# The last expert tile taken into the loop, its rows spread by 0/1 matrices on four row groups

## The reference, cut to what matters

```python
# hier_moe: top-1 of 4 expert groups, then top-2 of its 4 experts: two experts of 16 for every token
for g in range(N_EXPERT_GROUPS):
    a = jnp.einsum('btd,edf->btef', h, w1[g])            # 1024 -> 512
    b = jnp.einsum('btd,edf->btef', h, w3[g])
    hid = jax.nn.silu(a) * b * comb[:, :, g, :, None]    # comb: the weight of the token for the expert
    out = out + jnp.einsum('btef,efd->btd', hid, w2[g])  # 512 -> 1024
x = x + gt2 * out                                        # gate gt2, per channel
y = rmsnorm(x, normf_g)
```

## Time and profile before

| what | value |
| --- | --- |
| median of 3 runs | 1212.12 us |
| the profiled execution, its own time | 1218.64 us |
| its span in the trace | 1216.8 us |
| expert stage, from the first L1238 to the end of the span | 893.4 to 1216.8 us |
| loads of weights at full rate | about 912 to 1162 us |
| PE busy over the whole span | 95% |
| DVE busy over the whole span | 44% |

### The profile page before, as it was taken

How to read it: one execution, slowest core, us unless ns; L and a number is a source line. 1 busy time by engine, 2 the same in 40 slices (tenths; PEclk the granted TensorE clock), 3 DMA queues, 4 the chain that set the end, 5 groups by cost and what they waited for, 6 DMA issues and landing times.

```text
span 1216.8 us, 28304 instructions
## 1 busy us (share of the span) xinstructions
PE 1156.2 (95%) x11779; PEld 935.9 (77%) x11779; DVE 540.7 (44%) x1249; ACT 378.7 (31%) x680; POOL 176.9 (15%) x277
## 2 busy tenths in 40 slices
PE   3898999999999999999989999999989999999986
PEld 2687889888899898988759999999755655555542
DVE  1743555565655654553254434357741221111117
ACT  5422333232333332332044444432411222222113
POOL 0343344344444000000000000000030000000030
PEclk9999999999999999999979999999979999999998
DMA  9999878768846589666887888386559999999974
GB/s 310 360 337 369 313 264 317 269 229 278 300 168 224 185 330 333 208 218 237 323 319 279 287 299 291 90 241 255 210 208 397 410 398 394 390 397 382 392 202 116
DMA packets 169763, 350.63 MB, mean 288 GB/s; under 512 B 12179, under 2 KB 116779, under 8 KB 159398
## 3 DMA queue, kind: packets, MB, share of 16 engines
q1 hardware_dynamic: 156230, 326.84, 74.1%
q0 software_dynamic: 6304, 14.57, 4.1%
q10 hardware_dynamic: 7152, 8.13, 2.5%
HBM read 320.08 MB, written 117.50 MB: 360 GB/s over the span
## 4 chain that ended last, share of the span: by engine, by line
PE 75%; DMA 15%; DVE 5%; ACT 2%; issue 2%; ACTq 0%; SPq 0%; DVEq 0%
PE psum L886 44%; DMA xg<-x_rows 11%; PE psum L1238 7%; PE psum L1253 4%; PE psum L962 3%; PE psum L948 2%; PE psum L937 2%; PE psum L928 2%; PE psum L827 2%; PE psum L984 1%; DMA kvr<-in_cache_v_dram 1%; DMA wraw<-in_w_in_dram 1%; PE psum L1011 1%; PE psum L1230 1%; DMA adar<-in_w_ada_dram 1%
## 5 line engine op out<-in xcount | busy, mean ns | idle before, releaser
L886 PE MATMUL psum<-hHi,whi 128*128 128x272 f32 x1216 | 359.0, 295 | 2.1 <-DVE hLo L1639 2.0
L886 PE MATMUL psum<-hLo,whi 128*128 128x272 f32 x1216 | 351.5, 289 | 0.0
L886 PE MATMUL psum<-hHi,wlo 128*128 128x272 f32 x1216 | 349.7, 288 | 0.0
L886 PEld LDWEIGHTS psum<-hHi,whi 128*128 128x128 f32 x1216 | 229.1, 188 | 21.2 <-issue 16.4
L886 PEld LDWEIGHTS psum<-hHi,wlo 128*128 128x128 f32 x1216 | 229.4, 189 | 0.0
L886 PEld LDWEIGHTS psum<-hLo,whi 128*128 128x128 f32 x1216 | 228.7, 188 | 0.0
L1238 PE MATMUL psum<-e,xs 128*32 128x256 f32 x3072 | 179.4, 385 | 4.0 <-issue 2.6
L1591 DVE TENSOR_TENSOR wlo<-wraw,whi 128x1024 fp32r<-128x1024 f32 x100 | 131.9, 1323 | 73.7 <-ACT whi L1354 73.4
L1238 PEld LDWEIGHTS psum<-e,xs 128*32 128x32 f32 x3072 | 101.0, 111 | 73.6 <-issue 11.4
L1354 ACT ACTIVATE whi<-wraw 128x1024 fp32r<-128x1024 f32 x100 | 104.7, 1051 | 34.1 <-PE psum L886 21.5
L1253 PE MATMUL psum<-e,hT 128*32 128x256 f32 x1440 | 83.9, 381 | 0.0
(11 more groups left out here) (365 smaller groups left out, 1726.0 us busy)
## 6 DMA issues: line engine op xcount, KB each, us to landing
e<-in_w_dram SPq DMA_DIRECT2D x48, 2048.0 KB, 15.1
wraw<-in_w_in_dram SPq DMA_DIRECT2D x76, 512.0 KB, 5.4
out_dram<-in_cache_k_dram SPq DMA_DIRECT2D x32, 1022.0 KB, 9.4
out_dram<-in_cache_v_dram SPq DMA_DIRECT2D x32, 1022.0 KB, 7.8
adar<-in_w_ada_dram SPq DMA_DIRECT2D x36, 512.0 KB, 6.9
kvr<-in_cache_k_dram SPq DMA_DIRECT2D x8, 2048.0 KB, 9.2
kvr<-in_cache_v_dram SPq DMA_DIRECT2D x8, 2048.0 KB, 7.7
x_rows<-zrow SPq DMA_DIRECT2D x7, 1170.0 KB, 12.3
```

Of the source, the lines that this page charges most:

```text
L886: mm = pe.matmul(psum[:, t, 0:HALF], w[:, slot, k, :], x[:, k, cols], start=(k == 0 and n == 0), stop=(k == k_n - 1 and n == 2))
```

## The change

Every tile runs in the loop (`Fori(0, pairs)`), the last one too. The store of `yq` moves from the end of a tile to the start of the next one, one slot further on in `y_rows`; so tile 0 stores zeros, and the last tile's result is never stored. The 0/1 matrix is now `placeq`, made in every tile, for the three row groups of the tile and on all 128 partitions, whose four quarters hold the same rows. At the end each sum is made of 12 matmuls of 32 rows and 256 columns, one for each row group and column quarter; quarter c lies in partitions 32c to 32c+31 and goes to a PSUM bank of its own. A sum takes four half-used banks, so two fit at once.

```diff
 SP, before the loop
-            sp.dma_start(place[:, :], k_small[0:TS, 96 + TS:96 + TS + NT]).then_inc(late_in, 16)
+            sp.dma_start(tokens[:, :], k_small[:, 96 + TS:96 + TS + NT]).then_inc(late_in, 16)
 SP, behind the loop
+            sp.wait_ge(spread_pe, 2 * pairs)
+            sp.sem_inc(xg_in[0], 16)
 PE
-            def tile(jp, q, last=False):
+            def tile(jp, q):
-                pe.wait_ge(weigh_done, 10 * jp + (5 * q + 1))
+                pe.wait_ge(weigh_done, 18 * jp + (9 * q + 1))
...
-                if last:
-                    hidden_T(jp, q, 2)
-                    pe.wait_ge(e2_in[q], 16 * jp + 16)
-                    pe.wait_ge(hT_done, 6 * jp + (3 * q + 3))
-                    for n in range(2):
-                        for fc in range(FC):
-                            mm = pe.matmul(psum[0:TS, 6 + n, :], hT[:, fc, :],
-                                           e2[q][:, fc, 512 * n:512 * n + 512], start=(fc == 0), stop=(fc == FC - 1))
-                        mm.then_inc(ye_pe, 1)
-                    return
...
-            with pe.Fori(0, before_last) as jp:
+            with pe.Fori(0, pairs) as jp:
                 for q in range(2):
                     tile(jp, q)
-            tile(before_last, 0)
-            tile(before_last, 1, last=True)
+            pe.wait_ge(weigh_done, 18 * pairs + 1)
+            pe.wait_ge(xs_done, 2 * pairs + 1)
+            pe.wait_ge(ye_ev, 6 * pairs + 3)
+            pe.sem_inc(y_pe, 1)
             for i, tt in enumerate(LAST_ORDER):
                 n = P if tt < TILES else NS
-                if i == 4:
-                    pe.wait_ge(f_gate, 1)
-                if i >= 3:
+                if i >= 2:
+                    pe.wait_ge(f_mix, i - 1)
+                more = () if i < 2 else (ya[:, 1, 0], ya[:, 1, 1]) if i == 2 else (x2[:, tt, :],)
+                for g in range(TG):
+                    for c in range(4):
+                        part = slice(32 * c, 32 * c + 32)
+                        mm = pe.matmul(summed(i)[0:n, c, :], placeq[part, g, P * tt:P * tt + n], yq[part, g, :], start=(g == 0),
+                                       stop=(g == TG - 1 and not more))
+                if more:
                     pe.wait_ge(yg_in[tt], 32)
-                for c in range(2):
-                    cols = slice(512 * c, 512 * c + 512)
-                    mm = pe.matmul(psum[0:n, 2 * (i % 4) + c, :], place[:, P * tt:P * tt + n], yev[:, cols], start=True,
-                                   stop=(i < 3))
-                    if i >= 3:
-                        mm = pe.matmul(psum[:, 2 * (i % 4) + c, :], ident[:, :], x2[:, tt, cols], start=False, stop=True)
+                for src in more:
+                    for c in range(4):
+                        mm = pe.matmul(summed(i)[0:n, c, :], ident[:, :], src[:, DQ * c:DQ * c + DQ], start=False,
+                                       stop=(src is more[-1]))
                 mm.then_inc(y_pe, 1)
 ACT
+                act.wait_ge(xg_in[q], 16 * jp + 16)
+                act.wait_ge(ye_ev, 6 * jp + (3 * q + 3))
+                for n in range(4):
+                    act.dma_start(y_rows[...], yq[32 * n:32 * n + 32, :, :]).then_inc(ye_out, 16)
                 for g in range(TG):
                     act.wait_ge(a_pe, 6 * jp + (3 * q + g + 4))
                     act.activation(sil[:, g, :], psum[:, g, 0:P], ACT.Silu).then_inc(sil_done, 1)
...
-                act.wait_ge(ye_ev, 6 * jp + (3 * q + 6))
-                for n in range(4):
-                    act.dma_start(y_rows[...], yq[32 * n:32 * n + 32, :, :]).then_inc(ye_out, 16)
 DVE, before the loop
+            own(dve.memset(yq[:, :, :], 0.0))
+            dve.sem_inc(ye_ev, 3)
 DVE, in each tile
+                    dve.tensor_scalar(spread[:, :, 2], group[:, :], xg[:, q, 4:5], None, ALU.mult).then_inc(weigh_done, 1)
...
+                dve.wait_ge(weigh_done, 18 * jp + (9 * q + 7))
+                for g in range(TG):
+                    dve.tensor_scalar(placeq[:, g, :], tokens[:, :], fq[:, g, 2:3], None, ALU.is_equal).then_inc(weigh_done, 1)
 DVE, at the end
+            dve.wait_ge(yg_in[TILES], 32)
+            own(dve.tensor_tensor(accs[:, 0], accs[:, 0], accs[:, 1], ALU.add))
+            dve.wait_ge(y_pe, 2)
+            dve.tensor_tensor(quarters(accs[:, 0]), quarters(accs[:, 0]), summed(0)[0:NS], ALU.add).then_inc(f_mix, 1)
+            dve.wait_ge(y_pe, 3)
+            dve.tensor_tensor(quarters(x2[:, 0, :]), quarters(x2[:, 0, :]), summed(1), ALU.add).then_inc(f_mix, 1)
+            dve.wait_ge(yg_in[0], 32)
+            dve.wait_ge(f_mix, 2)
+            own(dve.tensor_tensor(x2[:, 0, :], x2[:, 0, :], ya[:, 0, 0], ALU.add))
+            dve.tensor_tensor(x2[:, 0, :], x2[:, 0, :], ya[:, 0, 1], ALU.add).then_inc(f_gate, 1)
+            own(dve.tensor_tensor(accs[:, 0], accs[:, 0], toks[:, 2, :], ALU.mult))
+            dve.wait_ge(y_pe, 4)
+            dve.tensor_tensor(quarters(x2[:, 1, :]), quarters(x2[:, 1, :]), summed(2), ALU.add).then_inc(f_mix, 1)
+            dve.wait_ge(f_mix, 3)
+            dve.sem_inc(f_gate, 1)
+            dve.tensor_tensor(x2[0:NS, TILES, :], x2[0:NS, TILES, :], accs[:, 0], ALU.add).then_inc(f_gate, 1)
```

More of the change, by code:

```diff
@@ L299, in _build @@
     xg = Region(h2_at)("xg", [TS, 2, ROW])
-    yev = Region(tokt_at)("yev", [TS, D])
+    r = Region(h2_at + 2 * ROW * 4)
+    tokens = r("tokens", [P, NT])
+    placeq = r("placeq", [P, TG, NT])
+    assert r.at <= lg_at
     e2 = (e2_0, e2_1)
@@ L308, in _build @@
     r = Region(base + P * 4)
-    gwq = Region(r.at)("gwq", [P, TG, DQ])
-    gw = r("gw", [TS, D])
-    diag = Region(r.at)("diag", [P, 2, P])
-    place = r("place", [TS, NT])
+    gwq = r("gwq", [P, TG, DQ])
+    r.at = base + P * 4 + D * 4
+    diag = r("diag", [P, 2, P])
+    r.at += P * 8
     slotq = r("slotq", [P, 2, 5])
@@ L320, in _build @@
     group = r("group", [TS, TG])
-    spread = r("spread", [TS, TG, 2])
-    fq = r("fq", [P, TG, 2])
+    spread = r("spread", [TS, TG, 3])
+    fq = r("fq", [P, TG, 3])
     assert r.at <= oT_at - 64
@@ L345, in summed, with quarters @@
     def summed(i):
[L347 removed]
+        return psum[:, 4 * (i % 2):4 * (i % 2) + 4, 0:DQ]
+    def quarters(t):
+        return t.rearrange("p (c d) -> p c d", d=DQ)
     win = w_in[0].rearrange("(k p) n -> p k n", p=P)
@@ L1523, in tile @@
                     act.activation(sil[:, g, :], psum[:, g, 0:P], ACT.Silu).then_inc(sil_done, 1)
-                if last:
-                    act.wait_ge(weigh_done, 10 * jp + (5 * q + 4))
-                    act.wait_ge(ye_ev, 6 * jp + (3 * q + 3))
-                    act.activation(gw[:, :], tokt[0:TS, 2, :], ACT.Identity, bias=factor[:, 1:2], scale=factor[:, 0:1])\
-                       .then_inc(g_done, 1)
-                    return
                 act.wait_ge(xgT_pe, 2 * jp + (q + 2))
@@ L2172, in tile @@
                 gated(2)
-                if last:
-                    turned_hidden(2)
-                    chosen_weight()
-                    dve.wait_ge(late_in, 128)
-                    dve.tensor_scalar(place[:, :], place[:, :], xg[:, q, 4:5], None, ALU.is_equal).then_inc(weigh_done, 1)
-                    dve.wait_ge(yg_in[0], 32)
-                    for r_ in range(2):
-                        own(dve.tensor_tensor(x2[:, 0, :], x2[:, 0, :], ya[:, 0, r_], ALU.add))
-                    dve.wait_ge(yg_in[TILES], 32)
-                    own(dve.tensor_tensor(accs[:, 0], accs[:, 0], accs[:, 1], ALU.add))
-                    dve.wait_ge(g_done, 6 * jp + (3 * q + 1))
-                    for n in range(2):
-                        cols = slice(512 * n, 512 * n + 512)
-                        dve.wait_ge(ye_pe, 6 * jp + (3 * q + n + 4))
-                        dve.tensor_tensor(yev[:, cols], psum[0:TS, 6 + n, :], gw[:, cols], ALU.mult).then_inc(ye_ev, 1)
-                    own(dve.tensor_tensor(accs[:, 0], accs[:, 0], toks[:, 2, :], ALU.mult))
-                    own(dve.tensor_tensor(x2[0:NS, TILES, :], x2[0:NS, TILES, :], accs[:, 0], ALU.add))
-                    return
                 chosen_weight()
-                dve.wait_ge(weigh_done, 10 * jp + (5 * q + 4))
-                dve.tensor_tensor(spread[:, :, :], factor[:, :].unsqueeze(1).to_broadcast([TS, TG, 2]),
+                dve.wait_ge(weigh_done, 18 * jp + (9 * q + 5))
+                dve.tensor_tensor(spread[:, :, 0:2], factor[:, :].unsqueeze(1).to_broadcast([TS, TG, 2]),
                                   group[:, :].unsqueeze(2).to_broadcast([TS, TG, 2]), ALU.mult).then_inc(weigh_done, 1)
@@ L2203, in tile @@
                     dve.tensor_tensor(yq[:, g, :], psum[:, 3 + g, 0:DQ], gwq[:, g, :], ALU.mult).then_inc(ye_ev, 1)
-            with dve.Fori(0, before_last) as jp:
+            with dve.Fori(0, pairs) as jp:
                 for q in range(2):
                     tile(jp, q)
-            tile(before_last, 0)
-            tile(before_last, 1, last=True)
```

(19 more changed lines are left out.)

63 lines of the change are left out of this document (27 added, 36 removed).

## The result

The changed kernel takes 1221.53 us (median of 20 runs), the kernel before 1213.87 us (median of 20 runs on the same chip): ratio 1.0061, 95% interval 1.0043 to 1.0078, or 7.4 us more. The forecast was 4.1 us more: the direction was right, the size too small. Set on the median that the prediction started from (1212.12 us), the ratio gives 1219.5 us, inside both stated ranges. It is slower by over 0.5%, the case that the prediction had given 0.22, and not within 0.5%, which had 0.68. The profiled executions take 1222.2 us (span; 1224.03 by their own time) against 1216.8.

What follows compares the result with a forecast made beforehand. It took PE, then the weight stream, to pace the loop, both hanging on SP's first load. +6.6 us in tile 0 and -2.5 at the end gave +4.1 on 1212.12: 1216.2 us; own range 1213 to 1220, with rivals 1207 to 1221.5.

Steps and rivals of the forecast that it cites:

- What bounds it: Expert loop: PE first, then the weight stream, both starting from SP's first load of the loop at 908.17 us.
- Part 1: Tile 0: ACT waits for the head load and issues four stores before sil(0), delaying the first load: +6.6 us.
- PE idles 4.6 us: Tile 0: PE's pause before hidden_T(0), moving the loop's first load from 908.2 to 912.8 us.
- The clock term: Tile 0: third inner runs partly at 1.2 GHz after PE's pause, +2.0 us, between 0 and 3.66.
- The sum 6.6: Tile 0: PE's 4.6 us pause plus 2.0 us of slower clock, between +4.6 and +8.3 us.
- In every tile but the first nothing changes: Later tiles: xg landed long before and the four stores keep their place between last yq and next sil; no cost.
- Part 2: Each tile: three DVE compares and a tiny multiply, 1.9 us, hidden under PE's outer 1 and 2; cost 0.
- Part 3: Last tile: after its inner PE works without a gap; last yq ends at 1190.8 us, 4.6 us earlier than yev.
- Part 4: The end: sums at 1.35 us with four row groups at once; last scaling at 1209.8, not 1212.25; gain 2.5 us.
- A: Last tile: code fetch causes the third inner's 6.5 us stall, so looping ends it; 1209.7 us; chance 0.20.
- B: Tile 0: head load lands before ACT needs it, so its wait costs 0; 1209.6 us; chance 0.06.
- C: The end's sums: row groups don't all work at once; 1236 us (none) or 1222.6 (two); chances 0.05 and 0.09.

Runs made afterwards that it cites:

- before_wait_only: Kernel before, with only ACT's wait for xg_in added at the start of each tile: 1220.87 us, ratio 1.0064 to the kernel before.
- store_at_end: Changed kernel with the store put back at the tile's end, slots as before, no zeros stored in tile 0: 1211.06 us, ratio 0.9991 to before.
- store_after_sil0: Changed kernel with ACT's wait and four stores moved behind sil(0) in each tile: 1220.17 us, ratio 1.0062 to the kernel before.
- store_at_end_2: Repeat of store_at_end, unchanged, on chip 3: 1205.51 us, ratio 1.0017 to the kernel before.
- gather_late: store_after_sil0 with POOL's gathers also waiting for the last tile's third inner: 1221.31 us, ratio 1.0069 to the kernel before.
- end_two_dmas: store_at_end with token tile 0 scaled earlier, samples third, SP issuing two 64-row output DMAs a token tile, not four of 32: 1241.49 us, ratio 1.0304 to before.

## Why the prediction was right, and where it was short

**What bounds it, right.** The prediction hung the loop on one event, SP's first load. One reading beside it was wrong: the 15 us of the earlier trace rows are the time of an `xg` load from issue to landing, and not PE's wait. The timeline of before has PE idle for 0.61 us there:

```profile
1159.32 0.88 PE L1230 MATMUL psum<-ident,xg 96*128 96x96 f32 x8 [0.61 <-DMA xg<-x_rows]
```

All such waits of the loop come to 3.8 us, so PE and the weight stream pace it nearly side by side. Nothing in the sum hung on that.

In the changed kernel that event moved by 7.7 us from the head's issue, and the span grew by 5.4 us: +7.7 in tile 0, +1.3 in the loop, -4.4 in the last tile, +1.4 at the end, and -0.6 because this execution reached the head earlier. I take that last one and the loop's for spread between executions; one trace of each kernel does not show it.

**Part 1, the mechanism right, the price 1.1 us short.** The wait for `xg_in[0]`, the four DMAs, `sil(0)` and PE's pause came in that order. The term "PE idles 4.6 us" measured 6.24. Of that 0.3 us had begun before the point where PE would have gone on, so `hidden_T(0)` came 5.9 us late, counted from the head's issue. Missing was ACT's table load, 1.28 us: 4.6 and 1.28 are those 5.9. It was there in the trace of before, 12 us ahead of the head's landing, and I had not read ACT's queue back that far: what stands ahead of the first activation moves with it. The Trainium skill (ScalarE activation tables: per-element evaluation and per-set limits, Table sets in the compiler and the runtime) has table loads placed per block; in every trace here one stands in the loop's body directly ahead of its first activation, and so behind any wait or DMA that is written before that. The clock term, 2.0, measured 1.58. The sum 6.6 became 7.7, inside the stated 4.6 to 8.3. That tile 0's store and wait make the loss is carried by before_wait_only and store_at_end. store_after_sil0 does not bear it out by time: without the stall in tile 0 it stayed at 1.0062, and only 4.1 to 4.6 us of its new loss were found. So what the moved store costs outside tile 0 is not settled.

**"In every tile but the first nothing changes", right for this kernel, but fragile.** The gathers start 2.15 us ahead of the last tile's third `inner` (2.20 before). Stores issued some 3 us later there made PE wait for a gather at the end on chip 2, with the clock 4.1 to 4.6 us; the prediction had not named this price.

**Part 2, right.** Three compares take 1.33 us in the last tile (1.9 forecast, with the multiply), and the last `yq` still waits 1.30 us for PE.

**Part 3, right.** 4.6 us forecast, 4.4 measured.

**Part 4, the gain by the wrong yardstick.** A sum cost 1.49 us (1.35 forecast), PE's last sum ended 15.1 us after the last `yq` (14.4) and the last scaling 19.9 us (19.0). I set the last scaling against the last scaling. But before, SP's 17 issues ended 1.8 us behind it, and now only 0.4. So a term of -1.4 and one of +0.9 were both missed, and what parts 3 and 4 give in the trace, 2.9 us, is near my 2.5 by luck. By the times of store_at_end and store_at_end_2 they give nothing that can be told from zero.

**Where the rest of the difference is.** 7.4 measured against 4.1 forecast: 1.1 in part 1, about 1.4 if parts 2 to 4 give the 1.1 us of store_at_end's ratio on chip 1 and not 2.5 (its median is 2.6 us under before, so this share is uncertain), and 0.8 that is under the interval of either ratio (2 us).

**The rivals.** A (the stall goes) was wrong: it came back with the same length in looped code with no fetch of code near it, and gather_late moved it with the gathers. B was wrong: ACT waited for the landing, and its first store came 3.71 us after the head's issue. C was wrong: 1.49 us a sum, under the 1.9 from which it decides. At the five changes between the 32-row and the 128-row form in the new end PE's rows leave no gap: each begins 0.07 us before the modelled end of the one ahead. Three sums of the prediction are off by little, and nothing hangs on them: `hid(0)` at 908.6 us by its terms (908.65 stated), 1207.7 for A without the clock loss (1207), 1229.6 for C (1229.8).

## What to carry to other kernels

A wait is not priced by itself: read the whole queue behind it, the function-table load included, and the clock of the PE that pauses for it; a pause of 4 to 7 us cost 1.6 to 2.3 us on top here. When a stage's end is compared, take the last event that anyone waits for (here the output issues), not the last piece of arithmetic. And before merging DMAs to save issues, look at the outermost dimension: from 32 to 2 cost 36 us (end_two_dmas beside store_at_end_2).

## What was unexpected of the hardware

- On two of four chips POOL's ten gathers cut PE's matmuls into bursts for some 6 us, wherever they fell, and ACT and DVE were released late as well (idle 6.94 and 4.51 us in the rows above); on the other two the same kernel ran clean, and the kernel before was 8 to 11 us faster. That this difference is the stall's is only argued.
- Removing 1.0 us of wait ahead of PE's next matmul returned 0.3 us; `inner` at the lower clock took 0.74 us more (one trace of each).
- With output DMAs issued by POOL the span ended 5.7 us behind its last issue, with SP's 2.1 us. The last of POOL's had landed 2.6 us behind it; the rest was POOL's DRAIN.
